# A second Strassen block in each pair of x panels, weight sums by adding DMAs, and X lending its places

## The reference

```
h = rmsnorm(x, norm_mix_g);  proj = h @ w_in                 # 2048 -> 6144
x = x + mixed @ w_o                                           # 2048 -> 2048
xq, xk, xv = hx @ w_xq, hm @ w_xk, hm @ w_xv;  x = x + xo @ w_xo
x = x + (silu(hf @ w_gate) * (hf @ w_up)) @ w_down
proj = h @ w_in_2;  g = sigmoid(h @ w_merge + b_merge)
merged = g_a * (y_a @ w_br_attn) + g_p * (y_p @ w_br_pool);  out = x + gate * rmsnorm_2(merged @ w_out, post_g)
```

## Time and profile before

| | us |
|---|---|
| median of three runs (lowest, highest) | 2067.9 (2067.67, 2068.31) |
| the profiled execution: its span | 2065.9 |
| TensorE busy in it | 2054.4 |
| VectorE busy | 1667.2 |
| ScalarE busy | 1181.2 |
| POOL busy | 50.0 |

### The profile page before, as it was taken

One profiled execution on the slowest core, in us unless ns is written; L12 is line 12 of the kernel. 1 busy time (PEld: TensorE's weight loads), 2 busy tenths in 40 slices (PEclk: granted clock), 3 DMA queues, 4 the chain that ended last, 5 costly groups with the idle time before them and its releaser, 6 DMA issues.

```text
span 2065.9 us, 25348 instructions
## 1 busy us (share of the span) xinstructions
PE 2054.4 (99%) x9334; PEld 1699.8 (82%) x9334; DVE 1667.2 (81%) x1830; ACT 1181.2 (57%) x1533; POOL 50.0 (2%) x84
## 2 busy tenths in 40 slices
PE   9999999999999999999999999999999999999998
PEld 8888888888888888888888888888788888888787
DVE  6877778867766788989889898898777778988875
ACT  7666557656655565555555555555756655654453
POOL 1000000000000000000000000000000000000000
PEclk9999999999999999999999999999999999999999
DMA  9555557655544458777777777776465567789763
GB/s 347 180 172 184 184 180 259 225 182 184 189 158 153 159 185 300 267 259 242 243 237 259 261 242 243 236 270 213 158 214 178 180 201 234 269 285 329 219 197 109
DMA packets 219259, 453.74 MB, mean 220 GB/s; under 512 B 14449, under 2 KB 17153, under 8 KB 219009
## 3 DMA queue, kind: packets, MB, share of 16 engines
q1 hardware_dynamic: 213232, 432.07, 62.9%
q0 software_dynamic: 5616, 19.94, 3.0%
q10 hardware_dynamic: 288, 0.13, 0.0%
HBM read 447.88 MB, written 4.19 MB: 219 GB/s over the span
## 4 chain that ended last, share of the span: by engine, by line
PE 95%; DVE 2%; ACT 1%; issue 1%; DMA 1%; POOL 0%; SPq 0%; DVEq 0%; POOLq 0%; ACTq 0%
PE ps L1117 30%; PE ps L1119 30%; PE ps L1118 29%; PE ps L687 2%; DVE wlo L2494 1%; PE ps L837 1%; PE ps L817 1%; PE ps L921 0%; DMA FR<-in_post_norm_g_dram 0%; PE ps L952 0%; PE ps L963 0%; PE ps L901 0%; DMA FR<-in_x_t_dram 0%; ACT whi L1718 0%; DVE raw L2507 0%
## 5 line engine op out<-in xcount | busy, mean ns | idle before, releaser
L2494 DVE TENSOR_TENSOR wlo<-raw,whi 128x1024 fp32r<-128x1024 f32 x835 | 1010.4, 1222 | 262.8 <-ACT whi L1718 257.4
L1718 ACT ACTIVATE whi<-raw 128x1024 fp32r<-128x1024 f32 x835 | 876.6, 1058 | 564.5 <-PE ps L1119 518.2
L1117 PE MATMUL ps<-whi,bh 128*128 128x512 f32 x1384 | 547.3, 395 | 2.3 <-DVE wlo L2494 2.1
L1119 PE MATMUL ps<-whi,bl 128*128 128x512 f32 x1384 | 539.9, 390 | 0.0
L1118 PE MATMUL ps<-wlo,bh 128*128 128x512 f32 x1384 | 539.2, 390 | 0.0
L1117 PE MATMUL ps<-whi,ah 128*128 128x512 f32 x1080 | 429.3, 398 | 0.2 <-DVE wlo L2494 0.2
L1119 PE MATMUL ps<-whi,al 128*128 128x512 f32 x1080 | 421.6, 390 | 0.0
L1118 PE MATMUL ps<-wlo,ah 128*128 128x512 f32 x1080 | 420.9, 390 | 0.0
L1117 PEld LDWEIGHTS ps<-whi,bh 128*128 128x128 f32 x1384 | 260.1, 188 | 57.0 <-DVE wlo L2494 3.1
L1119 PEld LDWEIGHTS ps<-whi,bl 128*128 128x128 f32 x1384 | 259.8, 188 | 54.7
L1118 PEld LDWEIGHTS ps<-wlo,bh 128*128 128x128 f32 x1384 | 260.2, 188 | 52.5 <-issue 0.2
(11 more groups left out here) (264 smaller groups left out, 1334.6 us busy)
## 6 DMA issues: line engine op xcount, KB each, us to landing
raw<-in_w_in_dram SPq DMA_DIRECT2D x168, 512.0 KB, 4.5
raw<-in_w_ada_dram SPq DMA_DIRECT2D x96, 512.0 KB, 4.6
raw<-in_w_gate_dram SPq DMA_DIRECT2D x88, 512.0 KB, 4.9
raw<-in_w_up_dram SPq DMA_DIRECT2D x88, 512.0 KB, 5.4
raw<-in_w_down_dram SPq DMA_DIRECT2D x88, 512.0 KB, 5.4
raw<-in_w_merge_dram SPq DMA_DIRECT2D x64, 512.0 KB, 5.0
raw<-in_w_o_dram SPq DMA_DIRECT2D x32, 512.0 KB, 4.8
raw<-in_w_xk_dram SPq DMA_DIRECT2D x32, 512.0 KB, 4.7
```

What stands on the lines that cost most here:

```text
L1117: e.matmul(o, xh[:, k, tokens], wh, start=first, stop=False, skip_group_check=more)
L1119: ins = e.matmul(o, xl[:, k, tokens], wh, start=False, skip_group_check=more, stop=kk == 1 and (st.end or st.form in READ))
L1718: done(e.activation(split_at(n)[0], place(item), ACT.Copy), "hi")
L2494: done(e.tensor_tensor(lo, place(stream.entries[n].item), hi.bitcast(F32), ALU.subtract), "lo")
```

## The change

1. **Two Strassen blocks in an x pair** (`QUADS`). Chunks 0 and 1 of both panels are each met by seven products, into the same banks. The second block needs sums of the activations of chunk 1 (form `x1`: `scale_x` scales XT[1] as well, four more ScalarE instructions in the same job; `make_forms("x1")` runs in `aside` after eight pauses). Of the pair's 22 entries 14 are of one tile.
2. **Adding DMAs** (`QUEUED`). In pairs whose first panel is tq, v, o, xk, xv, xq, xo, q, pu or out, the sums for M5 and M4 are made by a DMA from POOL's queue that adds in place; M6 and M7 stay on VectorE. M5's sum is placed 6 entries ahead (3 or 4 in some), not 2. `add_weights` calls are written between POOL's other work.
3. **X lends its places** (`SPARES = 4`). In the x stage X serves as four more places of `raw`, for items first used from entry 14 on; such a load waits until the eight squares of X are done. X is loaded a second time after the last of them, and its users wait for that.

```
+QUADS = {"tq": 2, "v": 2, "rg": 2}
+QUEUED = ("tq", "v", "rg", "o", "xk", "xv", "xq", "xo", "q", "ga", "pu", "gp", "out")
+SPARES = 4
@@ Stream._pair
+            product("M5", 0, start=True, job=False)
+            product("M5", 1, job=False)
+            product("M3", 0, start=True, job=False)
+            product("M3", 1)
+            normal(f, *next(todo), snap=("s5", q))
+            product("M1", 0, start=True)
+            product("M1", 1)
+            normal(f, *next(todo), snap=("s1", q))
+            product("M6", 0, job=False)
+            product("M2", 0, start=True)
+            product("M6", 1, job=False)
+            product("M2", 1, snap=("v", q))
+            normal(f, *next(todo))
+            product("M7", 0)
+            product("M7", 1)
+            normal(f, *next(todo), snap=("s3", q))
+            product("M4", 0, aside=q)
...
+            if quads == 2 and i == 0:
+                product("M4", 1)
...
+        early = 2
+        if self.panels[f - 1].stagger == "first":
+            early = 3 if queued else 1
+        elif queued:
+            early = 4 if q == 0 else 6
+        for k, made in enumerate(at):
+            for form, n in (("M5", made["M5"] - early), ("M6", made["M3"] + 1),
+                            ("M7", made["M1"] + 2 if quads == 1 else made["M6"] + 1),
+                            ("M4", max(made["M2"], made["M6"]) + 1)):
+                self.sums[made[form]] = Sum(n, made, k, form, queued and form in ("M5", "M4"))
@@ Stream._loads
+            fit = [r for r in range(number) if r < RAWS or (self.spares[r - RAWS].first <= first[item][0]
+                                                            and last[item][0] < self.spares[r - RAWS].last)]
+            at = min(fit, key=lambda r: (-1, r < RAWS) if holds[r] is None else last[holds[r]])
@@ scale_x
                     ins = e.activation(AF["x"][:, k, :], XT[0][:, k, :], ACT.Copy, scale=gcols("mix", 0)[k])
+                done(ins, "af")
+                for k in range(4):
+                    ins = e.activation(AF["x1"][:, k, :], XT[1][:, k, :], ACT.Copy, scale=gcols("mix", 1)[k])
@@ pool_program
             def root(name, of, src, dst):
+                add_weights(made_by_mean[of] - 1)
                 e.wait_ge(s["ms"], mean_n(of))
...
+            def add_weights(n):
+                while queued and stream.sums[queued[0]].before <= n:
+                    m = queued.pop(0)
+                    item, add = stream.entries[m]
+                    ready_to_sum(e, m)
+                    e.dma_start(place(item), place(add), accum_op=ALU.add).then_inc(sum_done(m)[0], 16)
@@ sync_program, load
                 if stream.before[i] is not None:
-                    wait_taken(stream.before[i])
+                    wait_taken(e, stream.before[i])
+                elif stream.place[i] >= RAWS:
+                    e.wait_ge(s["x_sq"], 8)
```

More of the change, by code:

```diff
@@ L77 @@
 Panel = namedtuple("Panel", "kind i w col rows stagger")
-Entry = namedtuple("Entry", "item add minus nth")
-Step = namedtuple("Step", "n p c hf tiles form start end made job taken snap aside")
+Entry = namedtuple("Entry", "item add")
+Step = namedtuple("Step", "n p c hf tiles form quad start end made job taken snap aside")
+Sum = namedtuple("Sum", "before pair quad form queue")
+Spare = namedtuple("Spare", "first last")
 PRODUCTS = {"M3": (0, 0, True, 1, 0), "M5": (0, 1, True, 1, 1), "M1": (1, 1, False, 0, 0),
@@ L266, in __init__ @@
             if entry.add is not None:
-                self.last_sum_of[entry.add] = entry.nth
+                self.sums_of.setdefault(entry.add, []).append(n)
+        self.sum_order = sorted(self.sums, key=lambda m: self.sums[m].before)
+        self.sum_signal, used = {}, {}
+        for m in self.sum_order:
+            one = self.sums[m]
+            name = f"sum_{one.form.lower()}{'ab'[one.quad]}" if one.queue else "sum_w"
+            used[name] = used.get(name, 0) + 1
+            self.sum_signal[m] = name, used[name] * (16 if one.queue else 1)
+        self.spares = [Spare(14, self.end_of[("rg", 1)])] * SPARES
         self._places()
@@ L280, in _add_ada, with _entry, _step @@
             self.items.append(("ada", *todo.pop(0)))
[L282 to L285, removed]
+    def _entry(self, item, add=None):
+        self.entries.append(Entry(item, add))
         return len(self.entries) - 1
-    def _step(self, n, p, c, hf, tiles, form=None, start=False, end=False, job=True, taken=True, snap=None,
+    def _step(self, n, p, c, hf, tiles, form=None, quad=0, start=False, end=False, job=True, taken=True, snap=None,
               aside=None):
-        self.steps.append(Step(n, p, c, hf, tiles, form, start, end, None, job, taken, snap, aside))
+        self.steps.append(Step(n, p, c, hf, tiles, form, quad, start, end, None, job, taken, snap, aside))
         if end:
@@ L317, in _pair @@
         chunks = len(self.panels[f].rows)
[L318 to L320 removed]
+        quads = min(QUADS.get(self.panels[f].kind, 1), chunks - 1)
+        places = [[self._item(p, c, hf) for p, hf in ((f, 1), (f, 0), (s, 0), (s, 1))] for c in range(quads)]
+        todo = iter([(c, hf) for c in range(quads, chunks) for hf in range(2)])
+        at = [{} for _ in range(quads)]
         def normal(p, c, hf, **more):
@@ L334, in _pair, with product @@
-        product("M1", b11, start=True, job=False)
-        if chunks == 4:
+        def product(form, k, start=False, **more):
+            b22, b12, b11, b21 = places[k]
+            item, add = {"M5": (b12, b11), "M3": (b22, None), "M1": (b11, None), "M6": (b22, b12), "M2": (b21, None),
+                         "M7": (b11, b22), "M4": (b21, b22)}[form]
+            at[k][form] = n = self._entry(item, add)
+            panel, tile, _, half, _ = PRODUCTS[form]
+            self._step(n, (f, s)[panel], k, half, (tile,), form, k, start=(start and k == 0), **more)
@@ L345, in _pair @@
[L345 to L349, removed]
+            product("M7", 0)
+            product("M7", 1)
+            normal(f, *next(todo), snap=("s3", q))
+            product("M4", 0, aside=q)
         todo = {"u": self._early, "d": self._early, "m": self._late}.get(self.panels[s].kind, [])
-        for i, (c, hf) in enumerate((c, hf) for c in range(1, chunks) for hf in range(2)):
+        for i, (c, hf) in enumerate((c, hf) for c in range(quads, chunks) for hf in range(2)):
@@ L354, in _pair @@
             normal(s, c, hf)
[L355 to L360, removed]
+            if quads == 2 and i == 0:
+                product("M4", 1)
+        self.pairs.append(((f, s), at[-1]))
+        queued = self.panels[f].kind in QUEUED
+        early = 2
[8 more added lines that the diff above has]
+                self.sums[made[form]] = Sum(n, made, k, form, queued and form in ("M5", "M4"))
     def _places(self):
@@ L438, in form_of @@
 def form_of(key):
-    return f"h{key[1]}" if key[0] == "h" else key[0]
+    return key[0] if key[0] != "h" and not key[1] else f"{key[0]}{key[1]}"
 def build_program(nc, a, out):
@@ L1729, in scalar_program @@
                 jobs.start(job)
+            for job in (pause(8), make_forms("x1")):
+                aside.start(job)
             for i, st in enumerate(stream.steps):
@@ L2489, in make @@
                         add_ada(item)
-                    if n in stream.sums_before:
-                        sum_weights(stream.sums_before[n])
+                    for m in [m for m in stream.sum_order if stream.sums[m].before == n and not stream.sums[m].queue]:
+                        sum_weights(m)
                     hi, lo = split_at(n)
```

178 lines of the change are left out of this document (117 added, 61 removed).

## The result

The changed kernel takes 2089.9 us (median of four runs, 2087.48 to 2092.67) against 2068.1 for the kernel before on the same chip (2067.67 to 2068.49): a ratio of 1.0106 (95% interval 1.0092 to 1.012). The forecast was 2072.6 with a range of 2063 to 2084. The sign was right, the size was not.

What follows compares the result with a forecast made beforehand. TensorE was taken as the bound, busy 2054.4 of 2065.9 us. The terms -6.8 + 7.5 + 4 + 0 = +4.7 gave a span of 2070.6, and with runs 2.0 above it 2072.6 us, range 2063 to 2084.

Steps and rivals of the forecast that it cites:

- Part 1: TensorE in the five x pairs: the saved product removes 30 matmuls of 0.227 us, -6.8 us.
- Part 2: The start: scale_x's extra work, M5's earlier loads and waiting for X's squares delay entry 14; +7.5 us, from 5.6 to 10.5.
- the chain by the root: At the start: tq0's eviction waits for X's squares, and TensorE transposes tq0 before entry 13; said to agree with 5.6 us lost.
- Part 3: VectorE at the front of x pairs, 25.5 of 25.7 us busy: 0.8 us lost a pair, +4 us.
- Part 4: Adding DMAs: a sum takes 6.4 us against 9.3 of cover outside x, so no cost to TensorE, 0.
- In x pairs the four more places cover it.: Part 4's claim that X's lent places keep M4's sums by DMA from delaying loads in x pairs; cost 0.
- twice that if the target is read as well: At the start, engine time of M5's 512 KB adding DMA: 1.35 us as a plain copy, otherwise 2.7.
- the one in which sums by DMA hold the loads: Rival for the queued pairs outside x: sums over 9.3 us stall TensorE, +33 us at 11.5 each; chance 14%.
- what was to show me wrong: Entry 14 before 50 us, TensorE's waits in the pairs under 1 or over 8 us, or TensorE waiting after 290 us.

Runs made afterwards that it cites:

- light_sums: Changed kernel, but in the x pairs VectorE's sums for M6 and M7 cover 8 of 1024 columns; 2086.9 us, 1.0084 of the kernel before.
- queue_outside: Changed kernel with one Strassen block in the x pairs, no adding DMAs in the x stage and no places lent by X; 2067.1 us, ratio 0.9995.
- light_dmas: Changed kernel, but in the x pairs the adding DMAs for M5 and M4 cover 128 of 1024 columns; 2078.6 us, 1.005 of the kernel before.
- light_both: Changed kernel, but in the x pairs VectorE's sums cover 8 and the adding DMAs 128 of 1024 columns; 2071.8 us, 1.0016 of the kernel before.
- start_fixed: Changed kernel with x1 scaled later in its own job, M5's first-pair sums 2 entries ahead, X lent from entry 20; 2093.9 us, ratio 1.0122.
- later_places: Changed kernel, but X's places are lent from entry 20 on, not 14; 2088.7 us, 1.0102 of the kernel before.
- m4_vector: Changed kernel, but in the x pairs VectorE makes M4's sums while M5's stay adding DMAs; 2091.3 us, 1.0112 of the kernel before.

## Why the prediction was wrong, step by step

- **Part 1, -6.8:** right; 9304 matmuls, and the spacing outside the half clock is still 0.227 us.
- **Part 2, +7.5:** the mechanism was right, and the sum measured 5.2, the lower end (5.6) and a little below. Entry 13's load was to land at 43.8 and ScalarE took it up at 43.61; the squares were to end at 46.3 and end at 46.04; SP's load of X was to go out at 46.3 and went at 46.06; entry 14 was to start at 52.8 or later and starts at 52.37. ScalarE's rows, against the earlier trace rows:

```profile
43.61 1.06 ACT L1816 ACTIVATE whi<-raw 128x1024 fp32r<-128x1024 f32 x1 [0.49 <-DMA raw<-in_w_in_dram]
...
45.85 0.19 ACT L1242 ACTIVATION_READ_ACCUMULATOR junk<-X 128x1 f32 x1
47.34 0.69 ACT L1346 ACTIVATE FR<-ps,Z 128x512 f32<-128x512 f32 x1 [1.30 <-POOL Z L2652]
49.99 1.06 ACT L1816 ACTIVATE whi<-X 128x1024 fp32r<-128x1024 f32 x1 [1.96 <-DMA X<-in_w_in_dram]
```

  What I called the chain by the root is where TensorE really stood: its transposes of tq0 wait 2.8 us for the eviction (L2000), before entry 13.

```profile
48.26 0.63 PE L780 MATMUL ps<-ident,FR 128*128 128x128 f32 x4 [2.78 <-DVE FR L2000]
48.64 0.48 PE L1211 MATMUL ps<-whi,ah 128*128 128x512 f32 x1
...
52.37 0.50 PE L1211 MATMUL ps<-whi,ah 128*128 128x512 f32 x1 [0.28 <-DVE wlo L2602]
```

- **Part 3, +4:** near. TensorE's waits on VectorE's splits in the pairs make 5.5 us in seven, 1.3 at the longest, and `light_sums` gives back 5.0 (6.9 where the DMAs are light too). VectorE is busy 199.8 of 253.5 us, in the first 26 us 23.34, against 20.6 of 25.7 before.
- **Part 4, 0:** this is the step that failed, in its sentence "In x pairs the four more places cover it." Outside the x stage it held: TensorE's waits after 312 us are 1.0 and 0.8 us, and `queue_outside` is level. In the x pairs the DMAs' bytes cost 12.3 us (`light_dmas`); just before the worst stall SP waited 12.0 and 6.2 us for places that sums had to free. I had asked only whether a place comes free in time, and priced engine time just once, at the start ("twice that if the target is read as well", 2.7; measured 2.8). In the pairs 19 sums of 2.8 us are 53 us of the 16 engines, on top of 0.58 x 235 = 136; measured is 0.71 x 253 = 180. The average leaves room. But the sums wait for VectorE (4.9 and 5.1 us in the second pair), SP waits for the sums, and then three sums and nine loads want the engines at once. The Trainium skill's fit (DMA: Bandwidth & Descriptors, "Anatomy of one DMA — SWDGE (gpsimd) path"), 3.2 us as an estimate for a transfer of 512 KB, is under the shortest landing measured, 4.5.
- **Not in the sum at all:** the granted clock. Both stalls of over 2 us in the pairs came with 3.4 or 6.8 us at the 1.2 GHz level, 4.2 us lost in all; that makes a stall of 5.7 us one of 8.2. Nor had I counted side work that comes late for reasons of its own (L850, L1305, 3.3 us even in `light_both`). The error in the pairs adds up: forecast -6.8 + 4 = -2.8, measured +18.3, so 21.1 too little. Of that 12.3 are the DMAs' bytes with the clock in them, 5.9 what `light_both` still loses, 1.0 VectorE's part above my 4, and 1.9 what the two loads cost only together. At the start 2.3 were forecast too much, and 1.3 come back after the pairs.
- **The rivals:** the one in which sums by DMA hold the loads was the right kind, at 14%, but I placed it outside x, where it doesn't occur, and left x out. Of what was to show me wrong, TensorE's waits in the pairs came true: 16.7 us, over 8. That TensorE should not wait after 290 us was badly put: the kernel before waits 2.5 us there. After its pairs, from 312 us on, the changed kernel waits 1.8.

What stays open: 1.6 us of the pairs' loss; why the side work is late even in `light_both`; why M5 on VectorE beats M4 on VectorE by 5 us in the pairs (TensorE's waits on its splits are 5.5 against 8.7); what two blocks would do without the places lent by X, which no run has; and by how much one DMA more or fewer would move the stall in the second pair, which came and went as a whole.

## What to carry to other kernels

Price an adding DMA twice: as a latency against its cover, and as engine time (here 2.8 us, two loads' worth) in the burst of loads that its landing releases; a DMA share averaged over a stage hides that burst. Where a sum must be made somewhere, moving all of it between two engines that are both near their limit changes only the name of the wait: the product saved 6.8 us, while the sums of this stage cost 19.2 as they are and 21.1 all on VectorE (255.4 - 234.3). A mixture was cheaper here, 10.9 with M5 on VectorE and M4 on DMAs (245.2 - 234.3), and still more than was saved. When several causes stand in series, undoing one shows nothing, so undo all of them before one is cleared.

## What the runs showed of the hardware

- An adding DMA of 512 KB within on-chip memory occupies the 16 engines for 2.8 us (two kernels, 50 and 30 sums), and lands after 4.5 us at the least and 6.1 in the median, 12.3 at the most in the changed kernel and 13.8 in `start_fixed`. With 128 of the 1024 columns it lands after 2.3/2.8/8.0.
- Full engines move 388 GB/s in two windows of the earlier trace rows, 317 in the third, and 372 to 397 in the changed kernel (146 to 156 us), but 196 to 220 GB/s where adding DMAs are among them, a sum's bytes counted once.
- When TensorE waits, the granted clock can fall to 0.5 for 3.4 or 6.8 us (10.2 once, in `start_fixed`), with matmuls 0.427 us apart. Every wait of 5.3 to 5.9 us in the second pair (six traces) brought 6.8 us of it, which began before the wait ended (at 149.1 against 150.9 in the changed kernel). Waits of 2.2 to 3.3 us brought sometimes none (2.78 in the changed kernel, 3.25 in `later_places`, 2.41 in `m4_vector`), sometimes 3.4 (2.24 in the changed kernel) or 6.8 (3.07 in `m4_vector`). So nearly the same start can come out some 3 us later: entry 16 stands at 58.0 in the changed kernel and at 61.0 in `m4_vector`.
